# A three-block network on one core: the residual stream with tokens on partitions at the seams between its stages

## The chip, the cores and the metric

The kernel runs on one core of a Trainium2 chip. The engines are TensorE (PE), VectorE (DVE), ScalarE (ACT), GpSimd (POOL) and SyncE (SP), which issues DMAs here. The metric is the device time of one execution in microseconds (us).

## What is computed

One sequence of 1024 tokens with 1024 channels passes through five residual steps. Each has the same frame, cut here from the reference:

```python
def rmsnorm(x, g):
    y = xf * lax.rsqrt(jnp.mean(xf * xf, axis=-1, keepdims=True) + RMS_EPS)
    return y * g

h = rmsnorm(x, mix_pre_g[layer])
m = even_mixer(h, ...)            # layer 0: attention and pooling, ends with @ w_out
m = odd_mixer(h, ...)             # layer 1: gated linear recurrence, ends with @ w_out
x = x + rmsnorm(m, mix_post_g[layer])
h = rmsnorm(x, ffn_pre_g[layer])
x = x + rmsnorm(swiglu(h, w_gate, w_up, w_down), ffn_post_g[layer])
...
xn = rmsnorm_2(h, norm_pre_g)     # second block: mLSTM and S5 branches, merged
h = h + rmsnorm_2(merged @ w_o, norm_post_g)
```

All values are float32. A mean over channels stands in each norm, ten of them in all: one behind each of five steps, one ahead of each of five.

## The kernel before

The activations lie with channels on the 128 partitions: `Y` and `X` are 8 tiles of 128 channels by 1024 tokens. Every large GEMM is made from three products of high and low parts (`H_hi`, `H_lo`, weights `w_hi`, `w_lo`), each a matmul with 512 moving columns. Weights come as 265 chunks of 128x1024 through three slots: SP loads a chunk into `raw`, POOL splits it into `w_hi` and `w_lo` (`split_chunks`), PE uses it and counts the semaphore `multiplied`. A chunk in a GEMM over all tokens (`columns`) is 48 matmuls: 8 channel tiles of input, 2 halves of the tokens, 3 products.

The program is a list of stages, and each engine runs its part of every stage in that order: `prelude` (constants of S5 and the recurrence, on DVE and ACT), `b0`, `fox` (attention), `b1`, `ffn(0)`, `b2`, `lru`, `b3`, `ffn(1)`, `b4`, `s5`, `mlstm`, `merge`, `b5`. The six calls of `boundary`, here called seams, hold the norms. With channels on partitions the mean over channels crosses the partitions. So ACT squares a tile, POOL sums up the squares or PE adds them with a matmul against `pick` (L441), ACT takes the root and DVE its inverse of an 8x128 piece, and PE spreads that over 128 partitions (L448). Then DVE scales `Y` (L515), DVE and POOL in turn add it to `X` (L518, L487), the sum is squared and summed up again for the norm ahead of the next stage, DVE scales again (L535), ACT copies out `H_hi` and DVE or POOL subtracts `H_lo` (L529, L495). The first GEMM of the next stage takes each `H` tile as it comes. `x` is kept in HBM between the seams as one tensor of 4 MB.

Each step ends with a GEMM into `Y`. In `fox` and `merge` it is eight column chunks of the output weight, 48 matmuls each, and DVE copies the result (L966, L2392). In `ffn` and `lru` it is a sum over row blocks in a loop (`pe_down`, `pe_out`): 8 output tiles of 12 matmuls for each block, and DVE adds each to `Y` (L1037, L1310); the last block stands alone behind the loop.

## Time and profile before

| what | value |
|---|---|
| three runs | 3793.61, 3794.27, 3800.0 us, median 3794.27 us |
| the profiled execution | 3794.27 us, of which the span of the trace is 3791.4 us |
| PE busy | 3459.4 us of the span |
| granted TensorE clock, mean | 0.957 of full speed |

A line of a group gives engine, line of the kernel, operation, output and inputs, shapes, count, busy time, mean duration in ns of one, and the idle time of the engine ahead of it with what ended it. A line of the timeline gives start and duration in us. A line of the windows gives, behind the stretch and its length, the busy time of each engine with the count of instructions, the mean granted clock, the share of time that the DMA engines were busy, and GB/s.

### The profile page before, as it was taken

The numbers are of one execution on the slowest core, as the hardware profiler recorded it, in microseconds if no ns is written. First come the engines' busy times: TensorE is split into PE (matmuls) and PEld (weight loads), VectorE is DVE, ScalarE is ACT, GpSimd is POOL, SyncE is SP. The second block draws the span as 40 slices with busy tenths as digits, with TensorE's granted clock in tenths as the row PEclk, the third lists the DMA queues.
The fourth block names the chain that finished last, engine by engine and source line by source line (L and its number), as shares of the span: only waits on it lengthen the run. The fifth ranks groups of instructions, "written<-read, shape, count | busy, mean of one in ns | idle before, by whom it ended". The sixth has DMA issues, their size and how long they took to land. (4 is left out here: it accounts for less than half of the span.)

```text
span 3791.4 us, 40722 instructions
## 1 busy us (share of the span) xinstructions
PE 3459.4 (91%) x15904; PEld 2800.8 (74%) x15904; DVE 1776.6 (47%) x1746; ACT 731.2 (19%) x923; POOL 1540.6 (41%) x720
## 2 busy tenths in 40 slices
...
DMA packets 246568, 215.78 MB, mean 57 GB/s; under 512 B 7988, under 2 KB 213428, under 8 KB 246472
## 3 DMA queue, kind: packets, MB, share of 16 engines
...
## 5 line engine op out<-in xcount | busy, mean ns | idle before, releaser
L331 POOL TENSOR_TENSOR w_hi<-raw,one_col 128x1024 fp32r<-128x1024 f32 x265 | 528.2, 1993 | 1921.2 <-PE ps L345 1866.2
L343 PE MATMUL ps<-H_hi,w_hi 128*128 128x512 f32 x2848 | 1138.7, 400 | 89.1 <-DVE H_lo L529 23.6
L345 PE MATMUL ps<-H_hi,w_lo 128*128 128x512 f32 x2848 | 1119.4, 393 | 0.0
L344 PE MATMUL ps<-H_lo,w_hi 128*128 128x512 f32 x2848 | 1119.0, 393 | 0.0
L343 PEld LDWEIGHTS ps<-H_hi,w_hi 128*128 128x128 f32 x2848 | 541.5, 190 | 218.5 <-issue 49.5
L333 POOL TENSOR_TENSOR w_lo<-raw,w_hi 128x1024 fp32r<-128x1024 f32 x265 | 667.0, 2517 | 20.7
L345 PEld LDWEIGHTS ps<-H_hi,w_lo 128*128 128x128 f32 x2848 | 540.8, 190 | 115.0
L344 PEld LDWEIGHTS ps<-H_lo,w_hi 128*128 128x128 f32 x2848 | 541.9, 190 | 109.0 <-issue 1.9
L1037 DVE TENSOR_TENSOR Y<-Y,ps 128x1024 f32<-128x1024 f32 x176 | 213.0, 1218 | 183.0 <-PE ps L345 183.0
L343 PE MATMUL ps<-ffn_f_hi,w_hi 128*128 128x512 f32 x704 | 273.9, 389 | 0.0
L344 PE MATMUL ps<-ffn_f_lo,w_hi 128*128 128x512 f32 x704 | 273.9, 389 | 0.0
L345 PE MATMUL ps<-ffn_f_hi,w_lo 128*128 128x512 f32 x704 | 273.9, 389 | 0.0
L1027 DVE SCALAR_TENSOR_TENSOR ffn_f<-ffn_a,ps 128x1024 f32<-128x1024 f32 x44 | 53.7, 1221 | 363.4 <-PE ps L345 363.4
L1024 DVE SCALAR_TENSOR_TENSOR ffn_a<-ffn_th,ps 128x1024 f32<-128x1024 f32 x44 | 53.8, 1222 | 349.7 <-ACT ffn_th L1016 349.6
L1016 ACT ACTIVATE ffn_th<-ps 128x1024 f32<-128x1024 f32 x44 | 45.2, 1027 | 754.4 <-PE ps L345 754.4
L1029 DVE TENSOR_TENSOR ffn_f_lo<-ffn_f,ffn_f_hi 128x1024 fp32r<-128x1024 f32 x44 | 138.2, 3142 | 49.6 <-ACT ffn_f_hi L1018 49.6
L345 PEld LDWEIGHTS ps<-ffn_f_hi,w_lo 128*128 128x128 f32 x704 | 132.2, 188 | 27.5
L343 PEld LDWEIGHTS ps<-ffn_f_hi,w_hi 128*128 128x128 f32 x704 | 132.2, 188 | 27.4
L344 PEld LDWEIGHTS ps<-ffn_f_lo,w_hi 128*128 128x128 f32 x704 | 132.2, 188 | 27.4
L1018 ACT ACTIVATE ffn_f_hi<-ffn_f 128x1024 fp32r<-128x1024 f32 x44 | 46.7, 1062 | 482.5 <-DVE ffn_f L1027 482.5
L441 PE MATMUL ps<-b_sq,pick 128*8 128x128 f32 x720 | 89.8, 291 | 49.0 <-ACT b_sq L421 49.0
L441 PEld LDWEIGHTS ps<-b_sq,pick 128*8 128x8 f32 x720 | 68.4, 96 | 69.4 <-issue 27.9
...
## 6 DMA issues: line engine op xcount, KB each, us to landing
...
b_X<-x_dram SPq DMA_DIRECT2D x4, 4096.0 KB, 13.7
...
b_X<-in_x_t SPq DMA_DIRECT2D x2, 4096.0 KB, 13.3
```

The costliest lines, as they stand in the source:

```text
L331: pool.tensor_tensor(w_hi[s][:, :n], raw[s][:, :n], one_col[:, :].broadcast_to([P, n]), ALU.mult).then_inc(split_hi, 1)
L333: pool.tensor_tensor(w_lo[s][:, :n], raw[s][:, :n], f32(w_hi[s][:, :n]), ALU.subtract).then_inc(split, 1)
L343: pe.matmul(o, l_hi, r_hi, start=first, stop=False)
L344: pe.matmul(o, l_hi, r_lo, start=False, stop=False)
L345: return pe.matmul(o, l_lo, r_hi, start=False, stop=last)
L441: ins = e.matmul(sums[stat], pick[:, m * KT:(m + 1) * KT], squares[:, m * P:(m + 1) * P], start=start and m == 0, stop=stop and m == KT - 1)
L1016: e.activation(th[t][:, :], pair(2 * t), ACT.Tanh, scale=0.5).then_inc(tanh_done, 1)
L1018: e.activation(f_hi[par_][:, t, :], f[t][:, :], ACT.Copy).then_inc(f_hi_done, 1)
L1024: e.scalar_tensor_tensor(a[t][:, :], th[t][:, :], 1.0, pair(2 * t), ALU.add, ALU.mult).then_inc(gated, 1)
L1027: e.scalar_tensor_tensor(f[t][:, :], a[t][:, :], 0.5, pair(2 * t + 1), ALU.mult, ALU.mult).then_inc(f_full, 1)
L1029: e.tensor_tensor(f_lo[par_][:, t, :], f[t][:, :], f32(f_hi[par_][:, t, :]), ALU.subtract).then_inc(f_ready, 1)
L1037: e.tensor_tensor(Y[:, n, :], Y[:, n, :], pair(n % 4), ALU.add).then_inc(y_added, 1)
```

## The change

At the seams the stream lies with tokens on partitions: a tile of `Y` is 128 tokens by 1024 channels. The GEMMs that end a step take the activations as stationary operand and the weights as moving one (`token_rows`). A mean over channels is then a sum along one partition, which ACT makes as it squares (`accum_out`). The way back to channels on partitions, which the next stage needs, is a product with a diagonal: `turn` multiplies a 128x128 piece of `Y` (stationary) by a diagonal that holds the inverse roots (`diag`), so the scaling by token happens in the product, and the gain of the channel comes with the copy out of PSUM (`high` on ACT, `low` on DVE).

The rest of the rewrite:

- The last row block of `ffn` and `lru` is moved into the seam and goes by token tile (`pe_last`), with three pairs of PSUM banks in turn. The output GEMMs of `fox` and `merge` go in two passes over four token tiles each (`out_pass`); they load five of their eight weight chunks again, so each has 13 chunks.
- The first three chunks of the next stage are multiplied inside the seam: chunks 0 and 1 on the first half of the tokens while the second half is still normed, the rest behind it. A fourth slot of weights (`w_hi3`, `w_lo3`, `raw3`) takes the first of them.
- `x` is fetched and stored by token tile, 512 KB each, by DMAs that ACT issues. POOL adds it to `Y` (in `b5` DVE does so for tiles 5 and 7).
- `b0` loads `x` in two halves and transposes it on PE. The gains of the norms behind the steps are turned into rows at the start (`gain_rows`), and each seam loads its row to all partitions (`G`).
- `prelude` moves from the start of the program to the end of `fox`.
- `b5` turns the result back with transposes and stores it by token tile from a staging buffer.
- `Y` is set to zero behind the first block of `ffn`, and by POOL in `lru`. Some semaphores are put together.

```diff
+    def token_rows(pe, s, bank, i, l_hi, l_lo):
+        for k in range(2):
+            w, t = slice(k * HALF, (k + 1) * HALF), slice(i * P, (i + 1) * P)
+            last = product(pe, ps[:, bank, :], l_hi[:, k, t], l_lo[:, k, t], w_hi[s][:, w], w_lo[s][:, w], k == 0, k == 1)
+        return last
...
+            def square(source, c, i):
+                e.activation(junk[:, :], source, ACT.Square, accum_out=entry(c, i)).then_inc(q["squared"], 1)
                squares[0] += 1
                wait(e, "squared", squares[0])
...
+            def x_root(i):
+                x_is_made(e, i)
+                if pre:
+                    square(Y[:, i, :], 3, i)
+                    e.activation(entry(4, i), entry(3, i), ACT.Sqrt, scale=1.0 / D, bias=eps_col[:, :]).then_inc(q["x_root"], 1)
+                    e.dma_start(x_dram[i, :, :], Y[:, i, :]).then_inc(q["x_stored"], 16)
+                if post and i + 3 < KT:
+                    fetch(e, i + 3)
+            def high(h, k):
+                wait(e, "turned", KT * h + k + 1)
+                e.activation(H_hi[:, k, halves[h]], ps[:, 6 + k % 2, :], ACT.Copy, scale=col(pre, k)).then_inc(q["h_hi"], 1)
...
+            def turn(h, k):
+                ...
+                for i in range(4):
+                    ins = e.matmul(ps[:, 6 + k % 2, i * P:(i + 1) * P], Y[:, 4 * h + i, k * P:(k + 1) * P], diag[:, 4 * h + i, :], start=True, stop=True)
+                ins.then_inc(q["turned"], 1)
...
+            turn(0, 0)
+            turn(0, 1)
+            if adds:
+                wait(e, "y_tiled", KT)
+            for k in range(KT):
+                wait(e, "h_low", k + 1)
+                if k + 2 < KT:
+                    turn(0, k + 2)
+                for c in range(2):
+                    if k == 0:
+                        ready(c)
+                    step(0, c, k)
+                if not post and 2 <= k <= 5:
+                    token_tile(k + 2)
+            turn(1, 0)
+            turn(1, 1)
+            ready(2)
+            for k in range(KT):
+                step(0, 2, k)
+                if k + 2 < KT:
+                    turn(1, k + 2)
+            for c in range(3):
+                for k in range(KT):
+                    wait(e, "h_low", KT + k + 1)
+                    ins = step(1, c, k)
+                ins.then_inc(multiplied, 1)
...
+            def x_add(i):
+                wait(e, "y_scaled", i + 1)
+                wait(e, f"x{i % 3}", 16 * (i // 3 + 1))
+                e.tensor_tensor(Y[:, i, :], Y[:, i, :], Xs[i % 3][:, :], ALU.add).then_inc(q["x_made"], 1)
...
+            if adds:
+                splits(0, 2)
+            if post:
+                for g in groups:
+                    for i in g:
+                        if not by_dve(i):
+                            x_add(i)
+                    if burst and g[0] == 0:
+                        out["splits"](e)
+                        splits(0, 2)
...
+            def y_tile(i):
+                tile_done(e, i)
+                e.tensor_tensor(Y[:, i, :], Y[:, i, :], pair(out["pair"](i)), ALU.add).then_inc(q["y_tiled"], 1)
+            def scale(i):
+                wait(e, "y_root", i + 1)
+                o(e.reciprocal(entry(2, i), entry(1, i)))
+                e.scalar_tensor_tensor(Y[:, i, :], y_of(i), entry(2, i), G[:, :], ALU.mult, ALU.mult).then_inc(q["y_scaled"], 1)
+            def turning(i):
+                wait(e, "x_root", i + 1)
+                o(e.reciprocal(entry(5, i), entry(4, i)))
+                e.tensor_scalar(diag[:, i, :], ident[:, :], entry(5, i), None, ALU.mult).then_inc(q["turn_ready"], 1)
...
+            for g in groups:
+                for n in range(len(g) + 3):
+                    if adds and n < len(g):
+                        y_tile(g[n])
+                    if 1 <= n <= len(g):
+                        scale(g[n - 1])
+                        if by_dve(g[n - 1]):
+                            x_add(g[n - 1])
+                    if pre and n >= 3:
+                        turning(g[n - 3])
+                    if pre and g[-1] == KT - 1 and n >= len(g) - 1:
+                        for _ in range(max(1, n - len(g) + 1)):
+                            low(*todo.pop(0))
```

What PE has in its row at seam `b2` before, from the last matmul of the FFN on: `b_t` and `b_sq` are sums and squares, `pick` the operand that sums them, `b_spreads` the one that spreads the inverse roots.

```order
L345 MATMUL ps<-ffn_f_hi_142,w_lo_55 128x512
L441 MATMUL ps<-b_t_158,pick 8x128 [waits ffn_y_added,boundary_y_summed]
L441 MATMUL ps<-b_t_158,pick 8x128 x7
L441 MATMUL ps<-b_sq_156,pick 8x128 [waits boundary_y_squared]
L441 MATMUL ps<-b_sq_156,pick 8x128 x7
L448 MATMUL ps<-b_inverses,b_spreads 128x128 [waits boundary_inverted,boundary_spreads_made]
L448 MATMUL ps<-b_inverses,b_spreads 128x128 x7
L441 MATMUL ps<-b_sq_155,pick 8x128 [waits boundary_squared]
```

And after, at the same place; `b_diag` are the diagonals, `w_hi_57` and `w_hi_51` chunks 0 and 1 of the next stage:

```order
L358 MATMUL ps<-w_hi_53,ffn_f_lo_141 128x512
L523 MATMUL ps<-b_diag,Y 128x128 [waits boundary_turn_ready]
L523 MATMUL ps<-b_diag,Y 128x128 x7
L523 MATMUL ps<-b_diag,Y 128x128 [waits boundary_h_low,boundary_y_tiled]
L523 MATMUL ps<-b_diag,Y 128x128 x3
L356 MATMUL ps<-H_hi,w_hi_57 128x512 [waits chunk_split]
L357 MATMUL ps<-H_lo,w_hi_57 128x512
L358 MATMUL ps<-H_hi,w_lo_58 128x512
L356 MATMUL ps<-H_hi,w_hi_51 128x512 [waits chunk_split]
L357 MATMUL ps<-H_lo,w_hi_51 128x512
L358 MATMUL ps<-H_hi,w_lo_54 128x512
```

The matmuls that only sum and spread are gone, and products with the diagonal stand between the steps of the next GEMM.

DVE at `b2` before, from the last tile of the FFN on:

```order
L1037 TENSOR_TENSOR Y<-Y,ps 128x1024 [waits chunk_multiplied]
L502 RECIPROCAL b_inverses<-b_roots 8x128 [waits boundary_rooted,ffn_y_added]
L510 UNCONDITIONAL_BRANCH [waits boundary_x_loaded,boundary_all_summed]
L510 ISA
L515 ISA
L515 SCALAR_TENSOR_TENSOR b_t_157<-Y,par,ps 128x1024
L514 ISA
L515 ISA [waits boundary_x_odd]
L515 REGISTER_ALU
L515 SCALAR_TENSOR_TENSOR b_t_158<-Y,par,ps 128x1024
```

And after, one round of the loop over tiles in the middle of the seam, and the start of the next; `b_stat` holds the sums and roots by token, `b_G` the gains:

```order
L629 TENSOR_TENSOR Y<-Y,ps 128x1024 [waits boundary_tile_done]
L633 RECIPROCAL b_stat<-b_stat 128x1 [waits boundary_y_root]
L636 SCALAR_TENSOR_TENSOR Y<-Y,b_stat,b_G 128x1024 [waits dve_order]
L645 RECIPROCAL b_stat<-b_stat 128x1 [waits boundary_x_root]
L646 TENSOR_SCALAR b_diag<-ident,b_stat 128x128 [waits dve_order]
L629 TENSOR_TENSOR Y<-Y,ps 128x1024 [waits boundary_tile_done]
```

For each tile DVE now adds, scales and makes a diagonal in one row of work, where the tiles of the FFN were added first and the scaling began behind the last of them.

POOL in the seam `b2` after: two chunks of the next stage, then the additions of `x`, of which the first two are shown.

```order
L344 TENSOR_TENSOR w_hi_57<-raw_63,one_col 128x1024 [waits chunk_multiplied,chunk_loaded3,ffn_y_added]
L346 TENSOR_TENSOR w_lo_58<-raw_63,w_hi_57 128x1024 [waits chunk_hi]
L344 TENSOR_TENSOR w_hi_51<-raw_60,one_col 128x1024 [waits chunk_multiplied,chunk_loaded0]
L346 TENSOR_TENSOR w_lo_54<-raw_60,w_hi_51 128x1024 [waits chunk_hi]
L604 TENSOR_TENSOR Y<-Y,b_X_149 128x1024 [waits boundary_x0,boundary_y_scaled]
L604 TENSOR_TENSOR Y<-Y,b_X_150 128x1024 [waits boundary_x1,boundary_y_scaled]
```

Before, POOL summed squares there, added four tiles to `X` and made four tiles of `H_lo`; the chunks stood between.

## Rows read from the trace of the kernel before

**Rows 1.** The page, busy time of each engine over the span.

```profile
PE 3459.4 (91%) x15904; PEld 2800.8 (74%) x15904; DVE 1776.6 (47%) x1746; ACT 731.2 (19%) x923; POOL 1540.6 (41%) x720
```

**Rows 2.** Windows: the stretches between the GEMMs at the six seams (PE, PEld, DVE, ACT, POOL busy, clock, DMA).

```profile
0.00:51.40 51.40, 17.62 (x144) 13.92 (x144) 21.74 (x97) 14.14 (x16) 17.33 (x27) 0.97 0.39 126
576.10:614.40 38.30, 24.16 (x192) 19.28 (x192) 21.16 (x19) 12.35 (x13) 24.01 (x10) 0.82 0.32 123
1339.40:1379.50 40.10, 24.89 (x192) 19.31 (x192) 21.38 (x19) 12.35 (x13) 26.11 (x11) 0.83 0.35 132
1746.50:1789.00 42.50, 27.06 (x192) 21.32 (x193) 21.19 (x19) 12.35 (x13) 27.49 (x12) 0.76 0.34 124
2512.00:2550.60 38.60, 23.15 (x193) 18.29 (x192) 21.59 (x19) 12.35 (x13) 26.18 (x11) 0.86 0.27 109
3755.90:3791.40 35.50, 9.18 (x49) 6.68 (x48) 16.42 (x14) 1.67 (x3) 16.50 (x6) 0.58 0.29 118
```

**Rows 3.** Windows: the first GEMMs behind two seams, and a steady stretch of the FFN.

```profile
51.40:85.00 33.60, 31.75 (x128) 24.80 (x129) 16.82 (x13) 13.28 (x12) 14.86 (x9) 0.95 0.16 50
1379.50:1415.00 35.50, 31.64 (x127) 24.33 (x128) 28.96 (x18) 9.48 (x9) 22.82 (x9) 0.96 0.06 15
700.00:750.00 50.00, 50.00 (x222) 41.42 (x221) 15.24 (x11) 2.09 (x2) 19.11 (x9) 1.00 0.18 53
```

**Rows 4.** Timeline of PE: float32 products of 128x128 by 128, and transposes.

```profile
2685.88 3.81 PE L1549 MATMUL ps<-s_U,s_turned 128*128 128x128 f32 x32 [1.39 <-ACT s_turned L1681]
100.99 1.09 PE L725 MATMUL ps<-ident,v_t 128*128 128x128 f32 x8 [1.11 <-ACT v_t L807]
```

**Rows 5.** Groups by form: the nearest instructions to those that the change adds.

```profile
L1037 DVE TENSOR_TENSOR Y<-Y,ps 128x1024 f32<-128x1024 f32 x176 | 213.0, 1218 | 183.0 <-PE ps L345 183.0
L410 ACT ACTIVATE b_sq<-Y 128x1024 f32 x40 | 42.4, 1061 | 232.1 <-POOL b_t L476 104.0 <-DVE Y L1037 67.4 <-DVE Y L966 29.3
L515 DVE SCALAR_TENSOR_TENSOR b_t<-Y,par,ps 128x1024 f32<-128x1024 f32 x40 | 49.4, 1276 | 18.3 <-PE ps L448 15.5 <-DVE b_X L518 2.8
L914 DVE SCALAR_TENSOR_TENSOR q_loB<-ps,q_hiB 128x512 fp32r<-128x512 f32 x4 | 2.8, 691 | 4.7 <-ACT q_hiB L822 4.7
L950 DVE RECIPROCAL fox_stat<-fox_stat 128x1 f32<-128x1 f32 x64 | 10.4, 163 | 47.9 <-ACT p L856 47.8
L476 POOL TENSOR_TENSOR b_t<-b_t,b_sq 128x1024 f32<-128x1024 f32 x35 | 83.9, 2398 | 33.5 <-ACT b_sq L410 30.0 <-POOL b_t L476 3.0 <-POOL b_t L472 0.5
L331 POOL TENSOR_TENSOR w_hi<-raw,one_col 128x1024 fp32r<-128x1024 f32 x260 | 522.5, 2010 | 1896.5 <-PE ps L345 1841.5 <-DMA raw<-in_w_in 39.7 <-DMA raw<-in_ev_w_in 14.4
L333 POOL TENSOR_TENSOR w_lo<-raw,w_hi 128x1024 fp32r<-128x1024 f32 x260 | 660.6, 2541 | 20.4
```

**Rows 6.** Timeline of DVE and POOL side by side, in the attention and in s5.

```profile
122.83 2.39 POOL L333 TENSOR_TENSOR w_lo<-raw,w_hi 128x1024 fp32r<-128x1024 f32 x1
123.91 0.16 DVE L950 RECIPROCAL fox_stat<-fox_stat 128x1 f32<-128x1 f32 x1 [0.99 <-ACT p L856]
124.11 1.46 DVE L951 TENSOR_SCALAR p<-p,fox_stat 128x640 f32<-128x640 f32 x1
...
2585.46 0.18 DVE L1836 TENSOR_TENSOR s_mag<-mag 128x16 f32<-128x16 f32 x1
2585.72 1.06 POOL L1476 TENSOR_TENSOR s_aB<-s_pw,s_bn 128x512 f32<-128x512 f32 x1 [5.90 <-DVE s_mag L1836]
2585.88 0.92 DVE L1839 TENSOR_TENSOR s_mag<-s_mag 128x16 f32<-128x16 f32 x1
```

**Rows 7.** DMA issues: the load of all of x, 4 MB, us to landing last.

```profile
b_X<-in_x_t SPq DMA_DIRECT2D x2, 4096.0 KB, 13.3
```

**Rows 8.** Timeline of DVE: first and last of the 92 steps of the prelude.

```profile
4.24 0.17 DVE L1110 SCALAR_TENSOR_TENSOR pre_e<-par 128x8 f32<-128x8 f32 x1 [4.24 <-POOL ident_b L2416]
...
26.24 0.17 DVE L1159 TENSOR_TENSOR q_im<-q_im,pre_e 128x16 f32<-128x16 f32 x1
```

**Rows 9.** Windows: the first stretch of s5.

```profile
2566.00:2663.00 97.00, 86.48 (x431) 71.32 (x430) 90.36 (x124) 12.94 (x13) 67.20 (x39) 0.98 0.34 98
```

More of the change, by code:

```diff
@@ L143, in __init__ @@
                     n += 1
-            per = [slots.count(s) for s in range(SLOTS)]
+            per = [slots.count(s) for s in range(SLOTS + 1)]
             rank = [slots[:j].count(s) for j, s in enumerate(slots)]
@@ new lines, in wait, with entry, by_dve, x_is_made @@
+        def wait(e, name, n):
+            e.wait_ge(q[name], b[name] + n)
+        def entry(c, i):
+            return stat[:, c * KT + i:c * KT + i + 1]
+        def by_dve(i):
+            return not pre and i in (5, 7)
+        def x_is_made(e, i):
+            if by_dve(i):
+                wait(e, "x_made_dve", i // 2 - 1)
+            else:
+                wait(e, "x_made", i + 1 if pre or i < 5 else 6)
+        def tile_done(e, i):
+            if i < KT - 1:
+                wait(e, "tile_done", i + 1)
+            else:
+                e.wait_ge(*out["last"])
@@ new lines, in pool, with splits @@
+        def pool(e):
+            for w, v in free:
+                e.wait_ge(w, v)
+            def x_add(i):
+                wait(e, "y_scaled", i + 1)
+                wait(e, f"x{i % 3}", 16 * (i // 3 + 1))
+                e.tensor_tensor(Y[:, i, :], Y[:, i, :], Xs[i % 3][:, :], ALU.add).then_inc(q["x_made"], 1)
+            def splits(first, last):
+                if seam:
+                    split_chunks(e, seam[0], seam[1] + first, seam[1] + last)
+            if adds:
+                splits(0, 2)
+            if post:
+                for g in groups:
[5 more added lines that the diff above has]
+                        splits(0, 2)
+            if not post:
+                splits(0, 2)
+            splits(2, 3)
@@ new lines, in dve, with copy @@
+            if not post:
+                def copy(i):
+                    wait(e, "tile_done", i + 1)
+                    e.tensor_copy(Y[:, i, :], pair(entry_pair(i))).then_inc(q["x_made"], 1)
+                for i in range(4):
+                    copy(i)
+                    if i >= 2:
+                        turning(i - 2)
+                turning(2)
+                turning(3)
+                for k in range(4):
+                    low(0, k)
+                for i in range(4, KT):
+                    copy(i)
+                    low(0, i)
+                for i in range(4, KT):
+                    turning(i)
+                for k in range(KT):
+                    low(1, k)
+                return
@@ L550, in fox @@
+    def fox(tmp_free):
         STEPS, N = FOX_PAIRS * 2 * KT, "fox"
@@ L882, in act @@
             cat(3)
+            pl["act"](e)
         def dve(e):
@@ L1074, in dve @@
                     dve_down(e, B + 2 * i + u, loop, 6 * u + 4, i)
[L1075 to L1078 removed]
+        out = dict(adds=True, work=pe_last, pair=tile_pair, last=(multiplied, stream.number(tail, 1)))
+        return dict(sp=sp, pool=pool, pe=pe, act=act, dve=dve, out=out, free=[(y_added, KT * (B - l + FF_BLOCKS))])
     def prelude():
@@ L2388, in dve @@
             o.leave(2)
-            with e.Fori(0, 2) as i:
-                for c in range(4):
-                    e.wait_ge(multiplied, stream.number(O, c, i))
-                    e.tensor_copy(tile(Y, 4 * i + c), pair(c)).then_inc(out_ready, 1)
-        return dict(sp=sp, pool=pool, pe=pe, act=act, dve=dve, y_ready=(out_ready, 4),
-                    x_free=[(multiplied, stream.number(G, 3, 1))], sq_free=[(m_ready, KT + 2)])
+        out = dict(adds=False, work=out_pass, pair=tile_pair, last=(multiplied, stream.number(O, KT + 4)), splits=lambda e: split_chunks(e, O, KT))
+        return dict(sp=sp, pool=pool, pe=pe, act=act, dve=dve, out=out, free=[(m_ready, KT + 2)])
     def constants(e):
```

727 lines of the change are left out of this document (394 added, 333 removed).

## The prediction

> **What bounds the kernel now.** I read the page first: PE is busy 3459.4 of 3791.4 us [rows 1], so the kernel is bound by PE, and only PE's pauses and its side work can be won. The windows then say where these lie. At six places PE has no GEMM: 51.4 us at the start, 38.3, 40.1, 42.5 and 38.6 us at the four seams within, 35.5 us at the end, 246 us together [rows 2]. PE shows some 24 us of work in each of the four, but those are the matmuls that sum squares and spread roots; the reader should not take them for GEMM work. No engine is full there (DVE 21, ACT 12, POOL 24 to 27 of some 40 us): it is a chain. Behind the pause the next GEMM waits for its `H` tiles. A steady stretch does 222 matmuls in 50 us, 0.226 each, while behind `b2` 127 take 35.5 us, with a clock of 0.96 [rows 3]. Three chunks are 144 matmuls, so the third is done 35.5 + 17 x 0.226 = 39.4 us behind the GEMM's start. I use this mark, "three chunks done", since there the old and new rows of PE meet again. Behind the last GEMM of a step it comes at 40.1 + 39.4 = 79.5 us at `b2`; with the same 39.4, 77.7 at `b1`. At the start it comes at 85 + 16 x 0.226 = 88.6 us.
>
> **What each piece costs after.** A `turn` is four float32 products of 128x128 by 128. The nearest row has two instructions for each such product, 32 in 3.81 us, 0.119 each [rows 4]; a turn is 8 x 0.119 = 0.95 us, 16 turns 15.2 us for each of five seams. Transposing a token tile is 1.1 us [rows 4]. DVE: 1.22 for the sum of a tile from PSUM, 1.28 for the scaling, 0.16 for a reciprocal (0.20 until its user starts), 0.69 for a `low`, about 0.3 for a diagonal (estimate, a small operation) [rows 5, 6]. ACT: 1.06 for a square [rows 5], and I allow 0.45 for the accumulator and the root. POOL: 2.40 for an addition of two SBUF tiles, 2.0 + 2.5 for splitting a chunk, 4.3 where nothing disturbs it [rows 5]. The matmuls of the GEMMs are the same in number, and swapping the operands leaves their shape.
>
> **The point that decides the three seams behind a loop (`b2`, `b3`, `b4`).** Here `scale` reads `Y` and `G`, both in SBUF, and the diagonal is made from SBUF. Rows 6 show what DVE does beside POOL: a `TENSOR_SCALAR` on SBUF that starts at 124.11, while POOL's splitting runs to 125.22, takes 1.46 us and so ends 0.35 us behind it; a 128x16 operation of 0.18 us takes 0.92 when POOL started 0.16 us ahead. Operations with an operand in PSUM keep to 1218 ns over 176 instances [rows 5]. So DVE on SBUF and POOL take turns. In a round DVE does `scale`, then a diagonal; POOL starts adding `x` when `scale` ends. POOL started 0.08 us behind the DVE instruction that released it [rows 6]; the diagonal has a reciprocal ahead of it and can start 0.20 us behind that one's start, at best overlapped to 0.11. So POOL is first by a hair, the diagonal waits for the addition, and the next tile's sum waits behind the diagonal on DVE. A round is 1.28 + 0.08 + 2.40 + 0.3 + 1.22 + 0.20 = 5.5 us, against 2.72 us (12 matmuls) that PE needs for a tile. Tiles 0 to 2, without diagonals in the round, take some 3.7 each and start at 9.8, since POOL first splits two chunks: scaling ends at 9.8 + 2 x 3.7 = 17.2 for tile 2, + 4 x 5.5 = 39.2 for tile 6, and 44 for tile 7. PE's tiles are done at about 24, two late, and the first `low` stands on DVE behind the diagonal of tile 4: 42.5; the second at 47.4. From there PE runs: 7 x (0.95 + 6 x 0.226) = 16.2 for the first half, 8 turns and 8 steps 13.0, 24 steps 16.3: 92.9. I add 1.3 for POOL's start behind the sum of the block before and 2.5 for a clock that has dropped in the pause of some 16 us (0.83 over the old stretch, 0.96 behind it [rows 2, 3]). 96.7 against 21.8 + 79.5 = 101.3: `b2` wins 4.6 us, and `b3` I take alike.
>
> The Trainium skill, page "SBUF — State Buffer", section "Who interferes with whom", states this as a rule: GpSimd and a VectorE instruction with two SBUF inputs, or in a two-port mode such as `tensor_scalar` reaches, hold a shared pair of ports in turn for a whole instruction. The trace agrees [rows 6]. Without that rule the seam would be paced by the 2.72 us of PE and win about 16 us; with it, 4.6.
>
> **`b4`.** S5 behind it is DVE's: busy 90.36 of 97 us [rows 9]. DVE leaves the seam by the last `low` at about 77 + 1.3, before at 21.8 + 54 = 76. I count 0.
>
> **`b1`.** Here the result comes from PSUM, so `scale` needs no turn with POOL. PE's second pass waits for its fourth chunk: POOL adds four tiles first (4 x 2.5 behind scaling, done at +9), then splits, +13.5 and with waits +20 against 3 x 5.44 = 16.3: 3.8 us late. Behind the pass the first `low` comes at 8.5 (square 1.5, scale 1.5, additions of tiles 4 and 5, square of tile 5, copy 0.6, low 0.7), the first half ends at 29, then 13.0 + 16.3: about 59. 77.7 - 59 - 3.8 - 1 (clock) = 13.9. Against it stands the prelude: its 92 small steps took 26.4 - 4.2 = 22.2 us alone [rows 8]. Now they stand ahead of the seam on DVE, beside POOL's splits in the first pass, and each may wait up to 2.4 us. From about 496, POOL is busy to 520 and lets through some 15 to 30 of them; the rest, 65 x 0.21, and the roots' tables on ACT end at about 538, where tile 0 should be scaled by 531: PE waits 6 to 8 us, of which POOL's lateness is saved: 5. `b1` wins 9.
>
> **`b0`.** The prelude no longer stands ahead (it ended at 26.4 [rows 8]). 4 MB took 13.3 us [rows 7], so half of `x` with its share of the chunks is there at about 11. Four tiles go through PE, DVE, ACT and DVE in some 15 us: first product at 26. Then 10.9 of steps, 8 turns and four tiles of transposes 23.3 less the first two turns, 13.0, 16.3: 77, with 2.5 for the clock and 3 for waits 82.6 against 88.6: 6 won.
>
> **`b5`.** 35.5 us now. After: 3.8 late in the second pass and 1 in the first; then tiles 4 to 7 are scaled and added in turn (7.5), and PE turns eight tiles at 1.1 each, while 4 MB leave at 4 MB per 13.3 us from 2.4 us on: 17.5 to the end, allow 18. 35.5 - 4.8 - 18 = 12.7.
>
> **The sum.** 6 + 9 + 4.6 + 4.6 + 0 + 12.7 = 36.9. The profiled execution took 3794.27 us, its span 3791.4 and 2.9 around it, and it is the median too. 3794.3 - 36.9 = 3757.4; I say 3758. Five chunks more in two GEMMs cost POOL 10 x 4.3 us beside 2 x 87 us of PE, nothing but what is counted.
>
> **Rivals.**
> - The diagonal is first. Then a round is 1.28 + 0.3 + 0.1 + 2.40 = 4.1 us, six rounds save 8 us at `b2`, `b3` and about 7 at `b4`: 3735. For it: 0.11 against 0.08 us is no margin; against it: 0.20 is what the row shows without overlap. Chance 0.30.
> - The change hardly moves the time: waits that I put at 3 in `b0` and at 0 in `fox` and `merge` (a chunk late in the first pass, a load late, 512-byte runs of the output) take 5 us at each seam: 3787 to 3795. Nothing in the trace shows them. Chance 0.10.
> - Slower: the turns. Their price is read from one place at full clock. 80 turns stand on PE's own row, so 37 us are used up when one costs 0.95 + 0.46 = 1.41 us. The clock is at 1.2 GHz behind a pause (0.83 and 0.76 in mean at the seams [rows 2]); at half clock a turn is 1.9 us, and if all ran so, 3758 + 80 x 0.95 = 3834. Against it: 127 matmuls behind a pause lose only 0.04 of the clock [rows 3], and the mixture of turns and steps keeps PE full. Chance 0.09.
> - More than I forecast without the lock mattering at all: 3720 or less. Chance 0.05.
>
> **How the numbers follow.** My forecast has 0.46, with its own range 3746 to 3774. What a measurement here can tell is about 0.2%, 7.6 us. Below 3786.7: 0.46 + 0.30 + 0.05 = 0.81. Within: 0.10. Above 3801.9: 0.09. For 8 in 10 the range takes in the first rival and half of the second: 3728 to 3788.
>
> **What would show it.** Timeline of DVE at the seam behind the first FFN: rounds of 5.5 us, with diagonals (128x128) of 2 us or more; in the first rival diagonals of 0.3 and rounds of 4.1. PE: a pause of 16 us between the second turn and the first step there, 6 at `b1`. A turn of 0.95 us. DVE's small steps of the prelude stretched beside POOL. At the start the first product at 26. Wrong if `scale` doesn't wait for POOL, if a turn costs over 1.2 us, or if PE waits within the two passes.

## The result and the profile after

The changed kernel takes 3737.25 us (median of 4 runs, 3733.05 to 3738.96), the kernel before 3794.23: ratio 0.9845, 95% interval 0.9828 to 0.9862. That is 57 us faster. I had forecast 3758, with 3728 to 3788 as the range. The profiled execution took 3733.05 us, its span 3730.9.

The page first, busy time and count of each engine, which answers to [rows 1]:

```profile
PE 3430.9 (92%) x15717; PEld 2797.7 (75%) x15717; DVE 1823.3 (49%) x1853; ACT 772.4 (21%) x1119; POOL 1470.9 (39%) x691
```

PE has 187 instructions fewer and 28.5 us less to do; the span fell by 60.5. So a good half of the gain, 32 us, is idle time of PE. Windows of the stretches in which PE still has no GEMM, which answer to [rows 2] (engines PE, PEld, DVE, ACT, POOL, then clock, DMA share, GB/s):

```profile
0.00:25.88 25.88, 11.17 (x61) 10.03 (x62) 9.89 (x14) 10.62 (x18) 12.79 (x22) 0.93 0.96 329
519.22:524.60 5.38, 0.00 (x1) 0.03 (x1) 4.26 (x19) 5.27 (x11) 0.00 (x0) 0.80 0.81 284
573.77:581.64 7.87, 1.70 (x9) 1.73 (x9) 3.35 (x7) 6.50 (x14) 4.57 (x3) 0.71 0.64 239
1313.73:1332.20 18.47, 4.65 (x20) 4.39 (x21) 18.22 (x19) 10.64 (x24) 8.65 (x4) 0.61 0.56 201
1709.24:1726.80 17.56, 4.60 (x23) 4.33 (x24) 17.31 (x19) 9.90 (x21) 7.79 (x4) 0.71 0.54 192
2461.49:2480.80 19.31, 5.48 (x25) 5.22 (x25) 19.02 (x21) 11.43 (x26) 9.04 (x5) 0.58 0.57 204
3705.43:3730.90 25.47, 10.08 (x65) 9.05 (x63) 12.11 (x11) 5.67 (x8) 3.90 (x2) 0.73 0.65 185
```

The five pauses before the next GEMM were 38 to 51 us long and are now 8 to 26; a new one of 5.4 us lies inside the attention's output GEMM (519.22).

To see where the 60.5 us come from, I put my mark, "three chunks done", on both traces. In the new one it is the 78th matmul behind the last turn of a seam.

| mark | before | after | ahead by | won in this step | forecast |
|---|---|---|---|---|---|
| `b0` | 88.6 | 75.3 | 13.3 | 13.3 | 6 |
| `b1` | 653.6 | 628.0 | 25.6 | 12.3 | 9 |
| `b2` | 1418.9 | 1379.3 | 39.6 | 14.0 | 4.6 |
| `b3` | 1826.4 | 1775.7 | 50.7 | 11.1 | 4.6 |
| first sum of the mLSTM (`b4`, S5) | 2965.6 | 2904.9 | 60.8 | 10.1 | 0 |
| first step of `merge` (mLSTM) | 3593.9 | 3541.4 | 52.5 | -8.3 | none |
| end (`b5`) | 3791.4 | 3730.9 | 60.5 | 8.0 | 12.7 |

Every seam within won 10 to 14 us, and 8 us were lost in a stage whose code the change does not touch. These are single traces: the attention and the recurrence wander by some 4 us from one profiled run to another (the stretch from the mark of `b2` to that of `b3` took 396.4 in this trace and 399.5 in the first experiment's, with the same code there), so a step is known to about that.

**The seam behind FFN0.** Timeline of DVE, POOL and PE (start, duration): first the second chunk's split and the first scaling, then a round.

```profile
1297.52 1.89 POOL L344 TENSOR_TENSOR w_hi<-raw,one_col 128x1024 fp32r<-128x1024 f32 x1
...
1298.65 1.84 DVE L636 SCALAR_TENSOR_TENSOR Y<-Y,b_stat,b_G 128x1024 f32<-128x1024 f32 x1
1299.49 3.27 POOL L346 TENSOR_TENSOR w_lo<-raw,w_hi 128x1024 fp32r<-128x1024 f32 x1
...
1316.65 1.28 DVE L636 SCALAR_TENSOR_TENSOR Y<-Y,b_stat,b_G 128x1024 f32<-128x1024 f32 x1
1317.85 0.15 DVE L645 RECIPROCAL b_stat<-b_stat 128x1 f32<-128x1 f32 x1
1318.01 2.35 POOL L604 TENSOR_TENSOR Y<-Y,b_X 128x1024 f32<-128x1024 f32 x1 [2.69 <-DVE Y L636]
1318.04 2.40 DVE L646 TENSOR_SCALAR b_diag<-ident,b_stat 128x128 f32<-128x128 f32 x1
1320.36 1.21 DVE L629 TENSOR_TENSOR Y<-Y,ps 128x1024 f32<-128x1024 f32 x1
...
1321.68 1.28 DVE L636 SCALAR_TENSOR_TENSOR Y<-Y,b_stat,b_G 128x1024 f32<-128x1024 f32 x1
...
1325.53 1.78 PEld L523 LDWEIGHTS ps<-b_diag,Y 128*128 128x128 f32 x8 [12.23 <-DVE b_diag L646]
```

These are rounds of the form that I forecast. `scale` (L636) starts at 1316.65 and again at 1321.68: 5.03 us; the two rounds ahead of this one took 5.68 and 5.89. POOL starts the addition of `x` at 1318.01, the diagonal (L646) at 1318.04, 0.03 behind, and the diagonal ends 0.08 behind the addition: a 128x128 operation takes 2.40 us. PE has done the FFN at 1313.7 and waits 11.8 us for the fourth diagonal. The Trainium skill (page "SBUF — State Buffer", section "Who interferes with whom") says that the first of the two to issue gets the shared ports for its whole instruction and the other is blocked until then; the trace agrees, with 2.40 us for the diagonal. It goes the other way too: the split that starts at 1299.49 takes 3.27 us, where the one before it (1295.15) took 2.41, since the scaling, issued at 1298.65 while POOL was at its `w_hi`, went ahead of it.

**The mLSTM.** Timeline of DVE and POOL at the end of the first head, the changed kernel first:

```profile
3021.55 2.87 POOL L344 TENSOR_TENSOR w_hi<-raw,one_col 128x1024 fp32r<-128x1024 f32 x1
3022.82 2.68 DVE L2520 SCALAR_TENSOR_TENSOR ml_acc<-ml_c_full,par,ml_acc 128x1024 f32<-128x1024 f32 x1 [0.15 <-DVE ml_acc L2519]
3024.50 3.21 POOL L346 TENSOR_TENSOR w_lo<-raw,w_hi 128x1024 fp32r<-128x1024 f32 x1
3025.54 1.22 DVE L2522 SCALAR_TENSOR_TENSOR ml_tz<-ml_tz,ps 128x1024 f32<-128x1024 f32 x1
3026.79 2.00 DVE L2523 TENSOR_TENSOR ml_acc<-ml_acc,ml_tz 128x1024 f32<-128x1024 f32 x1
```

and the same operations before (L2520 is L2308 there):

```profile
3083.58 1.28 DVE L2308 SCALAR_TENSOR_TENSOR ml_acc<-ml_c_full,par,ml_acc 128x1024 f32<-128x1024 f32 x1 [0.15 <-DVE ml_acc L2307]
3084.90 1.22 DVE L2310 SCALAR_TENSOR_TENSOR ml_tz<-ml_tz,ps 128x1024 f32<-128x1024 f32 x1
3086.15 1.22 DVE L2311 TENSOR_TENSOR ml_acc<-ml_acc,ml_tz 128x1024 f32<-128x1024 f32 x1
```

The same two forms at the end of the last head before:

```profile
3551.96 2.68 DVE L2308 SCALAR_TENSOR_TENSOR ml_acc<-ml_c_full,par,ml_acc 128x1024 f32<-128x1024 f32 x1 [0.15 <-DVE ml_acc L2307]
...
3555.93 2.00 DVE L2311 TENSOR_TENSOR ml_acc<-ml_acc,ml_tz 128x1024 f32<-128x1024 f32 x1
```

Before, POOL had nothing to do here behind its first chunk in the first three heads. Now it splits a second one at once (3021.55), and DVE's `ml_acc` from `ml_c_full` takes 2.68 us where it took 1.28, the last one 2.00 where it took 1.22. PE waits for the result. That is 2.2 us for each of three heads, 6.5 of the 8.3; the last head took 2.68 and 2.00 before too, so nothing is lost there. The cause would be the table of slots. Chunks are dealt on over the three slots without a break now, and the chunk of a next head goes into a slot that was last used three chunks before; in the old table the first head followed S5's chunks at a distance of two, and the loop has one distance for all heads. POOL is allowed to start one chunk sooner, and does so into DVE's last operations.

**S5.** DVE's first operation of the stage, before and after:

```profile
2566.81 0.14 DVE L1808 MEMSET s_Kp<- 128x96 f32 x1 [2.55 <-POOL H_lo L495]
```

```profile
2511.96 0.14 DVE L2020 MEMSET s_Kp<- 128x96 f32 x1
```

DVE entered S5 54.9 us ahead, only 4.2 more than at the mark of `b3`, as I had reckoned from its busy row. Yet at the end of S5 the lead was 60.8.

**`b1` and `b5`.** The prelude's last step, the first scaling, and PE behind it:

```profile
522.34 0.17 DVE L1361 TENSOR_TENSOR q_im<-q_im,pre_e 128x16 f32<-128x16 f32 x1
522.55 0.16 DVE L633 RECIPROCAL b_stat<-b_stat 128x1 f32<-128x1 f32 x1
523.17 1.28 DVE L636 SCALAR_TENSOR_TENSOR Y<-ps,b_stat,b_G 128x1024 f32<-128x1024 f32 x1 [0.45 <-DMA b_G<-gains_dram]
524.60 0.77 PE L356 MATMUL ps<-w_hi,H_hi 128*128 128x512 f32 x1 [5.38 <-DVE Y L636]
```

and at `b5`, ACT's last root, its first copy to the staging buffer, and SP's stores:

```profile
3708.53 0.29 ACT L464 ACTIVATE b_stat<-b_stat,eps_col 128x1 f32<-128x1 f32 x1
3713.14 1.94 ACT L511 ACTIVATE b_staged<-ps 128x1024 f32<-128x1024 f32 x2 [4.32 <-DVE Y L641]
3714.19 11.70 SPq L445 DMA_DIRECT2D out<-b_staged  x8
```

ACT stands still from 3708.8 to 3713.1, though tile 0 lay in PSUM at about 3706.4; the first store is issued at 3714.19, 8.6 us behind PE's last GEMM matmul.

### The profile page after: what moved, and what is told of

It is laid out like the page before. It is cut to its first block and busy times, and to the rows that moved or that the text cites. A ratio compares the mean times of both kernels' runs of the same rounds, so it can differ in the third digit from the quotient of the medians.

```text
span 3730.9 us, 39655 instructions
## 1 busy us (share of the span) xinstructions
PE 3430.9 (92%) x15717; PEld 2797.7 (75%) x15717; DVE 1823.3 (49%) x1853; ACT 772.4 (21%) x1119; POOL 1470.9 (39%) x691
## 5 line engine op out<-in xcount | busy, mean ns | idle before, releaser
L358 PE MATMUL ps<-H_hi,w_lo 128*128 128x512 f32 x2720 | 1067.7, 393 | 0.0
L357 PE MATMUL ps<-H_lo,w_hi 128*128 128x512 f32 x2720 | 1067.1, 392 | 0.0
L346 POOL TENSOR_TENSOR w_lo<-raw,w_hi 128x1024 fp32r<-128x1024 f32 x275 | 693.2, 2521 | 21.6
L356 PE MATMUL ps<-w_hi,ffn_f_hi 128*128 128x512 f32 x704 | 274.1, 389 | 0.0
L357 PE MATMUL ps<-w_lo,ffn_f_hi 128*128 128x512 f32 x704 | 273.9, 389 | 0.0
L358 PE MATMUL ps<-w_hi,ffn_f_lo 128*128 128x512 f32 x704 | 273.9, 389 | 0.0
L1240 DVE TENSOR_TENSOR Y<-Y,ps 128x1024 f32<-128x1024 f32 x160 | 193.3, 1217 | 157.2 <-PE ps L358 157.2
L356 PEld LDWEIGHTS ps<-w_hi,ffn_f_hi 128*128 128x128 f32 x704 | 132.1, 188 | 27.9 <-DVE Y L629 0.5
L358 PEld LDWEIGHTS ps<-w_hi,ffn_f_lo 128*128 128x128 f32 x704 | 132.1, 188 | 27.5
L357 PEld LDWEIGHTS ps<-w_lo,ffn_f_hi 128*128 128x128 f32 x704 | 132.1, 188 | 27.4
L523 PE MATMUL ps<-b_diag,Y 128*128 128x128 f32 x640 | 95.3, 301 | 54.7 <-DVE b_diag L646 40.3
L523 PEld LDWEIGHTS ps<-b_diag,Y 128*128 128x128 f32 x640 | 90.6, 213 | 66.2 <-DVE b_diag L646 42.2
```

The source lines that it names most:

```text
L346: pool.tensor_tensor(w_lo[s][:, :n], raw[s][:, :n], f32(w_hi[s][:, :n]), ALU.subtract).then_inc(split, 1)
L356: pe.matmul(o, l_hi, r_hi, start=first, stop=False)
L357: pe.matmul(o, l_hi, r_lo, start=False, stop=False)
L358: return pe.matmul(o, l_lo, r_hi, start=False, stop=last)
L523: ins = e.matmul(ps[:, 6 + k % 2, i * P:(i + 1) * P], Y[:, 4 * h + i, k * P:(k + 1) * P], diag[:, 4 * h + i, :], start=True, stop=True)
L1240: e.tensor_tensor(rows, rows, ps[:, 2 * (n % 4):2 * (n % 4) + 2, :], ALU.add).then_inc(y_added, 1)
```

## Experiments

Each ratio is to the kernel before on the same chip, which was one for e1 to e4, another for e5 to e8 and a third for e9 to e11. An interval is about 6 us wide to either side (4 for e9), so for edits of a few us the trace decides and the time only has to agree.

| run | median us (lowest to highest) | ratio to before, interval |
|---|---|---|
| the change | 3737.25 (3733.05 to 3738.96) | 0.9845, 0.9828 to 0.9862 |
| e1, split held back | 3728.49 (3723.99 to 3729.88) | 0.9822, 0.9805 to 0.9838 |
| e2, diagonals on ACT | 3719.11 (3718.33 to 3720.56) | 0.9799, 0.9783 to 0.9816 |
| e3, diagonal first | 3721.91 (3719.88 to 3726.77) | 0.9811, 0.9794 to 0.9827 |
| e4, prelude in the FFN | 3735.35 (3732.79 to 3737.01) | 0.9841, 0.9824 to 0.9857 |
| e5, as e3, `b1` as it was | 3719.59 (3718.32 to 3721.37) | 0.9801, 0.9785 to 0.9817 |
| e6, as e5, a chunk earlier | 3714.26 (3713.14 to 3715.24) | 0.9786, 0.9770 to 0.9803 |
| e7, stores earlier | 3730.67 (3727.84 to 3734.46) | 0.9833, 0.9817 to 0.9850 |
| e8, as e4, POOL zeroes `Y` | 3733.15 (3730.21 to 3736.85) | 0.9840, 0.9824 to 0.9857 |
| e9, turns twice | 3796.33 (3794.48 to 3799.11) | 1.0000, 0.9991 to 1.0010 |
| e10, `x` of 8 columns | 3699.27 (3695.37 to 3699.99) | 0.9743, 0.9728 to 0.9758 |
| e11, e1, e6, e7 and e8 | 3701.62 (3698.92 to 3702.55) | 0.9752, 0.9738 to 0.9765 |

For the three seams behind a loop I give the length from DVE's first sum to the mark, 98.6, 99.0 and 96.9 us before, and the round as it is between the later tiles:

| kernel | round | `b2` | `b3` | `b4` |
|---|---|---|---|---|
| the change | 5.03 | 84.6 | 85.8 | 85.5 |
| e2 | 3.5 to 3.7 | 80.5 | 76.4 | 80.1 |
| e5 | 3.91 | 79.5 | 77.1 | 79.5 |
| e6 | 3.91 | 77.0 | 77.0 | 77.0 |
| e10 | 3.42 | 74.0 | 72.7 | 75.3 |

### e10: the addition without its size

```diff
-                e.tensor_tensor(Y[:, i, :], Y[:, i, :], Xs[i % 3][:, :], ALU.add).then_inc(q["x_made"], 1)
+                e.tensor_tensor(Y[:, i, 0:8], Y[:, i, 0:8], Xs[i % 3][:, 0:8], ALU.add).then_inc(q["x_made"], 1)
```

> POOL adds x in 8 of the 1024 columns of a tile, in the changed kernel, so the rest of x is left out of the sum; every instruction and wait stands where it stood. With DVE and POOL taking turns an addition of 2.40 us is in each round; without it a round is 1.21 + 0.15 + 1.28 + 0.15 + 0.3 = 3.1 us. Theory (the addition sets the round through the shared turns): 5.04 to 3.1 over five rounds is 9 to 10 us at each of b2, b3 and b4 and 2 to 4 at b1: 3706 (3700 to 3712), and a diagonal takes 0.3, not 2.4. Rival: DVE's own row or ACT's squares set the round, and the diagonals only show a wait for ACT: within 5 us of 3737.

It took 3699.27, 38 us less than the change and 0.7 below the theory's range. DVE in the seam behind FFN0:

```profile
1308.72 0.29 DVE L646 TENSOR_SCALAR b_diag<-ident,b_stat 128x128 f32<-128x128 f32 x1
1308.92 1.22 DVE L629 TENSOR_TENSOR Y<-Y,ps 128x1024 f32<-128x1024 f32 x1
1310.30 0.17 DVE L633 RECIPROCAL b_stat<-b_stat 128x1 f32<-128x1 f32 x1 [0.17 <-ACT b_stat L464]
1310.50 1.28 DVE L636 SCALAR_TENSOR_TENSOR Y<-Y,b_stat,b_G 128x1024 f32<-128x1024 f32 x1
```

The diagonal takes 0.29 us. With no edit to DVE's program its round fell from 5.03 to 3.2 here and 3.42 in the later rounds, and `b1` is 3.5 us shorter. ACT is what DVE waits for now (the next `RECIPROCAL` follows 0.17 behind the sum, on ACT's root). So POOL's addition, through the shared turns, set the round, as forecast.

### e3 and e5: the order of the first rival

```diff
                     if adds and n < len(g):
                         y_tile(g[n])
+                    if pre and n >= 3:
+                        turning(g[n - 3])
                     if 1 <= n <= len(g):
                         scale(g[n - 1])
...
-                    if pre and n >= 3:
-                        turning(g[n - 3])
```

> DVE makes a round's diagonal ahead of that round's scaling, not behind it: one line moved. This is the order of my first rival. Theory (taking turns): sum beside POOL, then diagonal 0.3 and scaling 1.28 between two additions of POOL's: 2.40 + 0.06 + 0.16 + 0.3 + 1.28 = 4.2 us for a round in place of 5.04; 0.85 x 5 = 4 us at each of b2 to b4: 3725 (3720 to 3730). Rival: the diagonal now stands ahead of the scaling that POOL's next addition waits for, and the reciprocal ahead of it waits for ACT's root: no gain or a loss, 3735 to 3745.

e3 took 3721.91. POOL's addition, the diagonal, `scale`, and the next addition:

```profile
1319.75 2.35 POOL L604 TENSOR_TENSOR Y<-Y,b_X 128x1024 f32<-128x1024 f32 x1 [1.56 <-DVE Y L636]
1320.91 1.28 DVE L646 TENSOR_SCALAR b_diag<-ident,b_stat 128x128 f32<-128x128 f32 x1
1322.30 1.28 DVE L636 SCALAR_TENSOR_TENSOR Y<-Y,b_stat,b_G 128x1024 f32<-128x1024 f32 x1
...
1323.66 2.35 POOL L604 TENSOR_TENSOR Y<-Y,b_X 128x1024 f32<-128x1024 f32 x1 [1.55 <-DVE Y L636]
```

A round is 3.91 us (additions at 19.75 and 23.66). The diagonal still waits for the addition, 1.28 us, but most of the addition now passes beside the sum from PSUM. Five rounds at 1.1 less give 5.6; the seam at `b2` is 5.2 shorter (79.4). At `b1` the order cost 4.6 us (from the end of the first pass to the mark 113.4 for 108.8; the 5.8 in the text that follows is the mark alone, of which 1.2 lay ahead of that pass's end). e5 leaves `b1` as it was:

> As the run with the diagonal ahead of the scaling, but at b2, b3 and b4 alone; b1, where that order cost 5.8 us on the trace, keeps the changed kernel's order. Theory: at b1 the result to be scaled is in PSUM, so DVE there has no turn to wait for and only stands still for the root when the diagonal is put first; the two effects add: 3722 less 5.8 gives 3716 (3713 to 3720). Rival: the loss at b1 belongs to the run, not to the order: 3720 to 3724.

On the trace `b1` is back (108.9); the time fell only 2.3 us, to 3719.59, within the theory's range but 0.4 below the rival's, and within what two runs can differ by. So it is the trace that tells the two apart.

### e2: diagonals on ACT

```diff
+                    if pre and n >= 3:
+                        wait(e, "x_inverse", g[n - 3] + 1)
+                        e.activation(diag[:, g[n - 3], :], ident[:, :], ACT.Copy, scale=entry(5, g[n - 3])).then_inc(q["turn_ready"], 1)
...
             def turning(i):
                 wait(e, "x_root", i + 1)
+                if post:
+                    e.reciprocal(entry(5, i), entry(4, i)).then_inc(q["x_inverse"], 1)
+                    return
```

> At b1 to b4 ACT makes the diagonals (a 128x128 copy of the identity with the inverse root as scale), DVE only the reciprocal. Theory (DVE on SBUF and POOL take turns, and that sets the round at the seam): with no SBUF operation of DVE behind the scaling, the round falls from 5.04 to 1.28 + 2.40 = 3.7 us; tile 7 is scaled 6 us sooner. 5 to 6 us at b2, b3 and b4, 2 at b1: 3719 (3714 to 3725). Rival: what sets the seam's end is the chain of turn, copy out and low on PE, ACT and DVE behind the tiles, and the diagonals only stand in it: the time stays within 4 us of 3737.

3719.11, as the theory said, but in part by luck: the three seams are 4.1, 9.4 and 5.4 us shorter where I had 5 to 6 for each, `b1` won nothing (109.2 for 108.8) where I had 2, and S5 took 3.8 us more. ACT and POOL:

```profile
1317.67 0.40 ACT L505 ACTIVATE b_diag<-ident,b_stat 128x128 f32<-128x128 f32 x1 [0.57 <-issue]
...
1318.18 2.36 POOL L607 TENSOR_TENSOR Y<-Y,b_X 128x1024 f32<-128x1024 f32 x1 [1.16 <-DVE Y L639]
...
1321.37 0.40 ACT L505 ACTIVATE b_diag<-ident,b_stat 128x128 f32<-128x128 f32 x1 [0.57 <-issue]
...
1321.71 2.36 POOL L607 TENSOR_TENSOR Y<-Y,b_X 128x1024 f32<-128x1024 f32 x1 [1.16 <-DVE Y L639]
```

The additions are 3.53 us apart. ACT's own row is full: one diagonal to the next is 3.70, with 0.57 idle in it, in which ACT issues the two DMAs for `x`. ACT would bound a shorter round, as in e10.

### e6: a chunk out of the seam

```diff
+            if adds and out["early"]:
+                split_chunks(e, seam[0], seam[1], seam[1] + 1)
             for w, v in free:
                 e.wait_ge(w, v)
...
-                splits(0, 2)
+                splits(1 if out["early"] else 0, 2)
```

> As the run before in this list, and POOL splits the chunk of the fourth slot at b2 and b4 without waiting for the end of the FFN's loop, 4.3 us of work moved out of the seam. Theory: POOL's first two additions, and ACT's squares behind them, come up to 4 us earlier, and DVE's first three scalings no longer take turns with a split (1.85 to 2.1 us in place of 1.28): 2 to 3 us at each of two seams, 3711 (3709 to 3715). Rival: from the third tile on the round is DVE's own, and an earlier start of POOL is lost in it: no difference, 3714 to 3718.

3714.26, which lies in the theory's range and in the rival's; the trace decides for the theory: both seams are 2.5 us shorter and equal now to `b3`. But S5 gave some of it back: from the mark of `b4` to the mLSTM's `xpad` it takes 374.8 us, where e5 takes 369.7. Which wait that is I have not settled; e2, whose `b4` was also shorter, has 374.2 there. By the first sum of the mLSTM, the mark of the table above, it is 380.0 for 376.2, and 380.8 in e2.

### e1: the mLSTM's split held back

```diff
+                if name == "ml" and j == 0:
+                    before = stream.number(name, j, i) - 2
```

> In each mLSTM head the first weight chunk of the next head may again be split only when the chunk two places ahead of it has been multiplied, as the kernel before had it; the changed kernel, whose slots are dealt on without a break, lets it be split one chunk sooner. Theory: the two chunks split in a row stand beside DVE's last operations of the head (a 128x1024 of 1.28 us takes 2.68, one of 1.22 takes 2.00), 2.2 us for each of four heads; against the 3737 us of the changed kernel this gives 3729 (3727 to 3731), and DVE at the merge stage stands 61 us ahead of the kernel before, not 52.5. Rival: the 8 us are the clock's or a DMA's, and the time stays at 3735 to 3739.

3728.49, and DVE at `merge` stands at 3536.2 from 2901.5 at the start of the mLSTM: 634.7 us, before 634.9, changed kernel 642.4. That is 57.7 us ahead of the kernel before, not 61, since the recurrence took 3 us more on this trace. DVE at the head's end:

```profile
3025.91 1.28 DVE L2522 SCALAR_TENSOR_TENSOR ml_acc<-ml_c_full,par,ml_acc 128x1024 f32<-128x1024 f32 x1 [0.15 <-DVE ml_acc L2521]
3027.22 1.22 DVE L2524 SCALAR_TENSOR_TENSOR ml_tz<-ml_tz,ps 128x1024 f32<-128x1024 f32 x1
3028.48 1.23 DVE L2525 TENSOR_TENSOR ml_acc<-ml_acc,ml_tz 128x1024 f32<-128x1024 f32 x1
```

These are the durations of before, in three heads; in the last, whose next chunk is that of `merge`, they stay at 2.68 and 2.00, as before. So it is three heads, not the four that I expected, and the stage got all 7.7 us back. The loss in the untouched stage is the slots' doing.

### e4 and e8: where the prelude stands

```diff
-            pl["dve"](e)
...
             dve_block(e, B, 0, first, 0, 0)
             dve_steps(e)(e.memset(Y[:, :, :], 0.0))
+            if l == 0:
+                pl["dve"](e)
```

> The prelude's steps stand on DVE and ACT in the first FFN behind its first block, not at the end of the attention. Theory: PE's wait of 5.4 us ahead of the second pass of the output GEMM (DVE scales tile 0 only at 523.2, behind the prelude) goes, and DVE has some 20 us to spare in the FFN: 3732 (3730 to 3734). Rival: the wait stays, since it is POOL's additions or the root's table load that make the second pass late, or the prelude now delays the second block of the FFN: 3736 to 3750.

3735.35: the theory's time was missed, and what happened is the rival's last point. The wait in `b1` of 5.4, with one of 1.1 behind it, became one of 2.8, and the mark of `b1` won 3.6; but from there to the mark of `b2` 6.3 were lost, 4.5 of them ahead of the seam. ACT's part of the prelude moves likewise. DVE's last prelude step, its next of the FFN, and PE:

```profile
679.92 0.17 DVE L1363 TENSOR_TENSOR q_im<-q_im,pre_e 128x16 f32<-128x16 f32 x1
680.36 1.22 DVE L1224 SCALAR_TENSOR_TENSOR ffn_a<-ffn_th,ps 128x1024 f32<-128x1024 f32 x1 [0.26 <-DVE q_im L1363]
...
682.99 0.29 PEld L356 LDWEIGHTS ps<-w_hi,ffn_f_hi 128*128 128x128 f32 x1 [3.17 <-DVE ffn_f L1227]
```

DVE had less room than I reckoned, since the zeroing of `Y`, 6.88 us, stands ahead of the prelude. e8 gives that to POOL:

```diff
+                e.memset(Y[:, :, :], 0.0).then_inc(sem("ffn_zeroed"), 1)
...
-            dve_steps(e)(e.memset(Y[:, :, :], 0.0))
+            if l == 0:
+                pl["dve"](e)
+                e.wait_ge(sem("ffn_zeroed"), 1)
+            else:
+                dve_steps(e)(e.memset(Y[:, :, :], 0.0))
```

> The prelude in the first FFN as before, and POOL sets Y to zero there in place of DVE, which frees DVE for 6.9 us just ahead of it. In the run with the prelude in the FFN the wait at b1 fell from 5.4 to 2.8 us, but DVE came from the prelude at 680.1 and PE had waited 2.7 us for it; b1's mark won 3.6 us and the FFN lost 6.2. Theory: DVE is back at 673, the FFN loses nothing: 3737 less 3.6 to 4.5 gives 3733 (3731 to 3735). Rival: POOL's 7 us of zeroing hold DVE off and stretch the prelude by as much, or a chunk comes late: 3735 to 3738.

3733.15; on the trace `b1` keeps its 3.4 us, and from there to the mark of `b2` 1.6 are lost in place of 6.3. The FFN itself loses nothing, as the theory said: 666.7 us to DVE's first sum of the seam, as in the changed kernel. The 1.6 lie in the seam behind it, where from the second `low` to the mark the granted clock is 0.95 and the stretch takes 45.9 us, for 1.00 and 44.3. So the prelude's place cost the change 2 us by the trace and 4 by the times, a small part of what the seams are about.

### e7: stores earlier

```diff
             def x_root(i):
+                if not pre and i + 3 >= KT:
+                    return
                 x_is_made(e, i)
...
-                for i in range(0, KT, 2):
+                for i in (0, 1, 2, 4, 6):
                     wait(e, "turned", i + 1)
```

> b5 alone: ACT copies tiles 0, 1, 2, 4 and 6 out of PSUM and no longer waits there for the sum of the last tiles, DVE copies 3, 5 and 7. In the changed kernel the first of the eight stores starts at 3714.4, and then the DMA engines are full to the end, 4 MB in 16.4 us. Theory: the first store is what is late, not the rate: it can start at 3709.8, and 4.6 us are won: 3732.6 (3731 to 3734). Rival: the stores are then held up by the turning of tiles 2 and 3, which waits for DVE: under 2 us, 3735 to 3737.

3730.67, 0.3 below the theory's range. ACT's three copies in a row, and SP's first store:

```profile
3708.42 3.00 ACT L515 ACTIVATE b_staged<-ps 128x1024 f32<-128x1024 f32 x3
3709.45 11.78 SPq L447 DMA_DIRECT2D out<-b_staged  x8
```

The store starts 4.7 us sooner, and from `merge` to the end the kernel takes 185.05 us for 189.55: 4.5. The stores themselves need 16.7 us in both.

### e9: the price of a turn

```diff
-                for i in range(4):
+                for i in (0, 1, 2, 3) * 2:
```

> Every turn is done twice into the same bank (8 more matmuls each, the result is unchanged). It measures the price on which my slower rival rests. In the changed kernel the turn takes PE 0.90 us between two steps at full clock, and 1.9 us for each of the first two behind the pause. Theory (turns stand fully on PE's own row once the first diagonals are there, at the price of the rows): 80 turns, ten of them behind a pause at up to 1.9: 70 x 0.90 + 10 x 1.4 = 77 us, 3814 (3805 to 3820), slower than the kernel before. Rival: in the first half of a seam PE waits for the copies out and the lows anyway, so that half of the turns costs nothing: 3772 to 3785.

3796.33, 59 us more than the change and just the time of the kernel before. Two turns between two steps:

```profile
1366.29 1.95 PE L523 MATMUL ps<-b_diag,Y 128*128 128x128 f32 x16
...
1369.47 0.72 PE L523 MATMUL ps<-b_diag,Y 128*128 128x128 f32 x5
```

A step with two turns is 3.18 us long, with one 2.27 (1336.80 to 1339.08 in the changed kernel): a turn between steps costs 0.9 as I had it. The mean over all 80 is 59 / 80 = 0.74: some stand in time in which PE waits anyway. Neither theory had this right. So turns of twice the price would have used up the whole gain.

### e11: all together

> Diagonal ahead of the scaling behind the loops, the chunk of the fourth slot split earlier, the mLSTM's split held back, the stores of b5 earlier, the prelude in the first FFN with POOL zeroing Y: five edits in one kernel. They lie in different stages. Theory (the effects add): 3714.3 for the first two, less 8.3, 4.5 and 3.7: 3698 (3694 to 3702). Rival: S5 or the attention gives some of it back, as S5 did with 4 us of the second edit: 3702 to 3708.

3701.62, 0.9752 of the kernel before, 94 us less. That is the upper end of the theory's range (3694 to 3702) and 0.4 below the rival's; its 3698 lies just below the lowest run. On the trace 5.4 us are missing from the mark of `b4` to `merge` (1010.2, in e1 1004.8). The rival had named S5, but only 2.3 of them lie there (378.8 for 376.5 to the first sum of the mLSTM); the other 3.1 are in the mLSTM, whose second head takes 157.2 us for 155.9. Why, I have not settled.

## Why the prediction was right, and where not

The time lies in the range, but 57 us were won where I had forecast 36, and the 3746 to 3774 that I had given my likeliest case alone were missed by 9 us. The mechanism of that case held, and yet the time came out at the first rival's 3735. That is not the rival being right: its rounds of 4.1 us and diagonals of 0.3 are not in the trace. It was reached through wrong sizes that mostly had one sign, and it is luck that they ended where the range had been widened for another reason. (The range took in 1 us of the second rival's 8, not the half of it that I wrote.)

- **Rounds at `b2` and `b3`.** Forecast 5.5 with diagonals of 2 us or more; measured 5.03 and 2.40 in the later rounds, where the diagonal ends 0.08 behind the addition, not 0.3 + 0.2. But the two rounds ahead of these take 5.68 and 5.89 at `b2`, 6.12 and 5.07 at `b3`: the four that I had at 22 us take 21.6 and 21.3. So the round was right in form and nearly in size, and under 1 us a seam comes from it. What I had the seam win without POOL's turns, 16 us, was too little: in e10 `b2` is 24.6 shorter than before.
- **The first scaling.** I had it wait until POOL had split both chunks (9.8 us behind the block's start). At `b2` and `b4` DVE takes its turn between two operations of POOL, and it starts at 6.6 (1298.65, the block having started at 1292.0). At `b3` it starts at 6.5, but there POOL had split the first of the two chunks ahead of the block. That is 3 us of each of three seams, most of the 4.4 by which the second `low` comes sooner at `b2` (43.0 for 47.4). This is the step of the working that failed: ports that change hands with each instruction were counted as held for POOL's whole queue.
- **The allowances.** I added 2.5 for the clock and 1.3 for POOL's start, which the 43.0 already holds. From the second `low` on (1335.03) the seam takes 44.3 us; I had 45.5 + 2.5. The clock in the pause is low (0.61), and the first two turns take 3.78 us for some 2.0, but that lies ahead of the second `low`. That nothing of it fell behind is luck in part: in e8 the same stretch had 0.95 and took 45.9. With the line above this is `b2`'s 9.4: 5.7 up to the second `low`, 1.2 and 2.5 behind it.
- **`b4`, forecast 0, won 10.** DVE did enter S5 only 4.2 us better off, as I said. What I missed is that being full for 97 us [rows 9] does not bind a stage of 393 us: over the stage DVE is busy 265 of 393 us before, and behind its full stretch it waits for PE in 79 of 297 us. PE stood 62.1 us ahead at the mark of `b4` (2590.0 before, 2527.9 after), so its lead can be had again at those waits. No run tests that, and e2, e6 and e11 show that S5 can also give 2 to 4 us back.
- **`b0`, forecast 6, won 13.3.** First product forecast at 26, measured 25.88. The 5.5 us of allowances behind it were not needed, and 49.4 us sufficed for 51.
- **`b1`, 9 and 12.3.** The wait on the prelude is 5.4, and one of 1.1 follows within the second pass, which I had named as a sign of being wrong; I had 3.8 and 5 for the two causes, 2.3 more. The seam behind the last GEMM matmul (571.8) takes 56.2 us, I had 60. Against that some 2 us went to the clock, which I had not counted there: ten matmuls behind the wait start 0.43 us apart, not 0.23. PE's pause behind the first turns is 6.2, as forecast.
- **`b5`, 12.7 and 8.0.** The passes came 2.2 us late, not 4.8. But I gave 17.5 to 18 us behind the last GEMM matmul, and it is 25.3: the first store goes out at 8.6, not 2.4, since ACT stands in its queue in front of its copy, waiting for a sum that it doesn't need (e7).
- **The mLSTM, not forecast, -8.3.** I read the split table for the seams alone, and took a stage that the change does not edit at nothing. It was the one term of the other sign that I had no rival for; e1 shows it to be the table's.
- **Where I was wrong about the place.** I put PE's pause between the second turn and the first step; it is ahead of the turns (11.8) and 2.0 behind them.
- **The slower rival** was priced right: 0.9 a turn between steps (e9), and a turn at double that would have brought the kernel back to the time before.

Sum of the differences: 7.3 + 3.3 + 9.4 + 6.5 + 10.1 - 8.3 - 4.7 = 23.6, against 60.5 - 36.9.

The runs test what paces the seams behind a loop, the stores, the prelude's place, the turns and the mLSTM. None takes the change back at one seam, so how the whole gain divides among the seams is read from single traces, and the gains of `b0` and `b4` rest on that reading alone.
